# Turning a modulation row in four parts behind four row tiles instead of in one piece

## The chip, the cores and the metric

One core of a Trainium2 chip runs the whole program. The metric is the device time of one execution in microseconds; the kernel before has a median of 3093.56 us over 3 runs (3090.25 to 3096.78). Engines: PE is TensorE, DVE is VectorE, ACT is ScalarE, POOL is GpSimd, SP issues nearly all DMAs.

## The reference, cut to what matters

Two layers over 384 tokens (128 context tokens with condition `c_ctx`, 256 latent tokens with condition `c`), width 1024. Every layer has a mixer and a retrieval block; in front of and behind each stands a modulation that is a linear map of the conditions:

```python
for l in range(DEPTH):                      # 2 layers
    mp = split(silu(c_ctx) @ mod_w[l] + mod_b[l], 6)      # mod_w: (2, 1024, 6*1024)
    ms = split(silu(c)     @ mod_w[l] + mod_b[l], 6)
    hp = rms_norm(xp, norm1_g[l]) * (1 + mp[1]) + mp[0]   # the same for xs with ms
    xp = xp + mp[2] * mixer_l(hp)
    hp = rms_norm(xp, norm2_g[l]) * (1 + mp[4]) + mp[3]
    xp = xp + mp[5] * peer(hp)

def peer(x):                                # per token, 8 heads
    q = x @ wq                              # 16 halves of 128
    sv, si = top_k(q . subkeys, 16)         # 128 sub-keys, two sides per head
    fv, fi = top_k(sv0 + sv1, 16)           # 16 of the 256 pairs -> 16 of 16384 experts
    g = softmax(fv)
    return sum(g * gelu(U[idx] . x) * V[idx])
```

So twelve modulation rows of 1024 numbers (six per layer) are needed for each of the two conditions. Rows 0 to 5 serve layer 0, rows 6 to 11 serve layer 1.

## The kernel before, in words

**Retrieval without a gather.** In each layer the kernel computes U[e].x for all 16384 experts in 128 *row tiles* of 128 experts (here "tile t"), with PE as the engine in question. fp32 numbers are split in a high and a low part, and three products are added: 24 matmuls of 128 x 384 columns per tile (`s_tile`, L1213 to L1223). What feeds a tile is a chain over four engines: SP loads a tile of U into URAW; DVE transposes it into UT (`turn_u`, L1567); ACT copies the high part into UHI (`u_hi`, L860); POOL subtracts to get the low part ULO (L659); PE multiplies. ACT then applies gelu to the tile's result (`gelu`, L865), and SP stores it. UT, UHI and ULO have two buffers each, and `u_hi` of tile t+2 waits until PE is done with tile t. So each engine can be at most about two tiles ahead.

**The selection beside it.** The first 72 of the 128 tiles of a layer stand beside the *selection*: DVE finds the top 16 of the sub-key scores, for three token tiles one after the other, 24 row tiles each. DVE's selection work is written out with calls of `next_u` between, which do the transposes. After tile 17 and tile 41 PE computes the scores of the next token tile (`tile_scores`, L1198), and after tiles 29 and 53 (and 79) it transposes the picks of the last one (`turn_picks`, L1210). Behind tile 72 come the gate matmuls (`gates`, L1233), 16 passes behind each tile, and after tile 127 the stage with V (L1246).

**The modulation rows of layer 1** are computed beside the selection of layer 0 ("the first selection"). Rows 6 to 11 take 12 tiles each. A row has four *products* (`next_mod` to `mod_product`, L982): after tile 12r, 12r+3, 12r+6 and 12r+9 PE multiplies the two conditions with 256 columns of `mod_w`, 8 matmuls with 32 output rows each that use four strips of the array; the profile shows each matmul as two passes. ACT copies the result to a quarter of MROW (L690). A product leaves the numbers along a row; the kernel needs them down the partitions. That is the *turn* (`next_mod_row`, L1009 to L1017): 8 matmuls, 16 passes, with MROW as weights and a two-column selector as the moving operand, into 16 columns of bank 7. ACT copies them to MODT (L696). Before the change the whole turn stands behind tile 12r+11, and the next row's first product behind tile 12r+12.

**Order and semaphores.** The order on every engine is written out by hand. PE signals a product by s_mrow, ACT its copy by s_mev; PE signals a turn by s_mtr, ACT its copy by s_mod. A turn waits for the row's four copies and for the MODT copy of the row before. ACT's copy of the next row's first product waits for s_mtr, since it overwrites MROW. SP loads the weights of product b+2 after product b, in four DMAs of 256 KB behind three tiles (`load_next_mod`, L396). `turn_picks` waits for s_mod, since it writes to bank 7 too.

**Layer 1** has the same selection, with nothing beside it. There the 72 tiles are run by loops (`s_tiles`, L351) on PE, ACT and SP; in layer 0 they are written out.

The loop over tiles on PE, before (L1256 to L1267):

```python
def s_tiles_beside(first, count):
    if l == 0:
        for six in range(first // 6, (first + count) // 6):
            r, i = divmod(six, 2)
            for j in range(6):
                s_tile(3 * six + j // 2, j % 2)
                if j % 3 == 0:
                    next_mod(r, i, j // 3)
            if i:
                next_mod_row(r)
    else:
        s_tiles(pe, first, count, s_tile)
```

Of the kernel before, what the change touches and what calls it, by code (L numbers as in the profile page):

```python
# [34 lines left out]
KC = D // P  # L35
# [41 lines left out]


S_LEVEL1, S_LEVEL2 = 18, 6
S_PICK = 6  # L80
BATCH = 8
HALF = 64
# [51 lines left out]
def build_step(nc, x_prompt, x_sample, cache_k, cache_v, c, c_ctx, mod_w, mod_b, norm1_g, norm2_g,  # L134
# [5 lines left out]
    with ctx:  # L140
# [188 lines left out]
        LATE0 = range(LATE00 + len(BESIDE), LATE1)  # L329
        LATE2 = range(LATE1 + NBT, MODSEGS * SEGB)  # L330
        pe_names = ["hm", "kv", "ktok", "rot", "s0", "s1"]
# [34 lines left out]
        def _(sp):  # L366
# [29 lines left out]
            def load_next_mod(b, part):  # L396
                sp.dma_start(MODR[:, b % 2, 2 * part:2 * part + 2, :], mod_w[1, :, bass.ds(b * MODB, MODB)]
                             .rearrange("(p k) m -> p k m", k=KC)[:, 2 * part:2 * part + 2, :]).then_inc(next_in[b % 2], 16)
# [66 lines left out]
            for u in range(2):  # L465
                load_a_out(u)
            load_late_mod(LATE0[0] + 2, MODSEGS * SEGB)
            for u in range(2, KC):
# [32 lines left out]
            for l in range(LAYERS):  # L501
# [18 lines left out]
                for k in range(2):  # L520
                    load_v(l, k, k)
                if l == 0:
                    for k in range(2):
                        sp.wait_ge(s_mrow, MODSEGS * SEGB - 1 + k)
                        for part in range(4):
                            load_next_mod(k, part)
                for k in range(2):
# [3 lines left out]
                n = TT * (S_LEVEL1 + S_LEVEL2)  # L531
                if l == 0:
                    blocks = MODSEGS * SEGB
                    for t in range(2, n):
                        s_step(l)(t // 2, t % 2)
                        b = t // 3 + 1
                        if 2 <= b < blocks:
                            if t % 3 == 0:
                                sp.wait_ge(s_mrow, blocks + b - 1)
                                load_next_mod(b, 0)  # L540
                                load_next_mod(b, 1)
                            else:
                                load_next_mod(b, 1 + t % 3)
                else:
                    s_tiles(sp, 2, n - 2, s_step(l))
                at = n
# [116 lines left out]
        def _(act):  # L663
# [20 lines left out]

            def next_mod(r, i, k):

                row = MODSEGS + r
                act.wait_ge(s_mrow, SEGB * row + 2 * i + k + 1)
                act.wait_ge(s_mtr, row)
                nc.scalar.activation(MROW[:, bass.ds(2 * MODB * i + MODB * k, MODB)], PS[:, 2, MODB * k:MODB * k + MODB], ACT.Copy)\  # L690
                    .then_inc(s_mev, 1)

            def next_mod_row(r):

                act.wait_ge(s_mtr, MODSEGS + r + 1)
                nc.scalar.activation(MODT[:, 1, KC * r:KC * r + KC, :],  # L696
                                     PS[:, 7, MODT_AT:MODT_AT + 2 * KC].rearrange("p (a b) -> p a b", b=2), ACT.Copy).then_inc(s_mod, 1)
# [116 lines left out]
            for b, (qt, j) in enumerate(BATCHES):  # L814
                n = P if qt == 0 else T
                if b + 1 < NBT:
                    exponents(b + 1)
                mpe.wait(act, f"t{b}")
                mact.mark(f"pt{b}", nc.scalar.activation(PROBT[:, :, 0:n], PS[:, 4:8, 0:n], ACT.Copy))
                mpe.wait(act, f"o{b}")  # L820
                rows = slice(64 * j, 64 * j + 64)
                mact.mark(f"oh{b}", nc.scalar.activation(HH[rows, 0:4, qt * P:qt * P + P],
                                                         PS[rows, 4, :].rearrange("p (a b) -> p a b", a=4), ACT.Copy))
                late_mod(LATE1 + b, 5)
            for b in LATE2:
# [7 lines left out]
            for l in range(LAYERS):  # L833
# [52 lines left out]
                def s_steps_beside(first, count):  # L886
                    if l == 0:
                        for six in range(first // 6, (first + count) // 6):
                            r, i = divmod(six, 2)
                            for j in range(6):  # L890
                                s_step(3 * six + j // 2, j % 2)
                                if j % 3 == 0:
                                    next_mod(r, i, j // 3)
                            if i:
                                next_mod_row(r)
                    else:
                        s_tiles(act, first, count, s_step)

# [69 lines left out]
        def _(pe):  # L968
# [32 lines left out]

            def next_mod(r, i, k):

                row = MODSEGS + r
                pe.wait_ge(next_in[k], 64 * (2 * r + i + 1))
                pe.wait_ge(s_mev, SEGB * row + 2 * i + k - 1)
                mod_product(2, k, k * MODB)

            def next_mod_row(r):  # L1009

                row = MODSEGS + r
# [137 lines left out]
            for b, (qt, j) in enumerate(BATCHES):  # L1149
                rows = slice(64 * j, 64 * j + 64)  # L1150
                nkt = 1 if qt == 0 else 3
                if b:
                    mdve.wait(pe, f"ol{b - 1}")
                    late_mod_left(LATE1 + b - 1)
# [17 lines left out]
                late_mod(LATE1 + b, 5)  # L1172
            for b in LATE2:
# [5 lines left out]
            mdve.wait(pe, "pl3")  # L1179
            late_mod_left(MODSEGS * SEGB - 1)  # L1180
            project_out("a_out")

            for l in range(LAYERS):
# [18 lines left out]
                def turn_picks(tile):  # L1202
                    g = TT * l + tile
                    pe.wait_ge(s_pick, g + 1)
                    if l == 0:
                        pe.wait_ge(s_mod, 1 + MODSEGS + (tile + 1) * MODSEGS // TT)
                    if g:
# [48 lines left out]
                def s_tiles_beside(first, count):  # L1256
                    if l == 0:
                        for six in range(first // 6, (first + count) // 6):
                            r, i = divmod(six, 2)
                            for j in range(6):  # L1260
                                s_tile(3 * six + j // 2, j % 2)
                                if j % 3 == 0:
                                    next_mod(r, i, j // 3)
                            if i:
                                next_mod_row(r)
                    else:
                        s_tiles(pe, first, count, s_tile)  # L1267

# [51 lines left out]
        def _(dve):  # L1320
# [169 lines left out]
            for g in range(4):  # L1490
# [3 lines left out]
                                                           in1=HH[:, 4 + g, :].bitcast(F32), op0=ALU.mult, op1=ALU.subtract))  # L1494
            modulation(0, EARLY, MODSEGS)
            los("a_out")
            to_residual("a_out", 0)

            for l in range(LAYERS):
                if l:  # L1500
                    modulation(1, 0, MODSEGS)
                    lo("c_in", 0, 1)
# [67 lines left out]
                def s_step(i, k):  # L1570
                    turn_u(i + 1, k)
# [35 lines left out]
                for tile in range(TT):  # L1607
# [53 lines left out]
                    assert turned[0] == 1 + (tile + 1) * (S_LEVEL1 + S_LEVEL2)  # L1661
                if l == 0:
                    dve.wait_ge(s_mrow, 2 * MODSEGS * SEGB)

# [127 lines left out]
```

## Time and profile before

| what | value |
|---|---|
| median of 3 runs | 3093.56 us (3090.25 to 3096.78) |
| profiled execution | 3099.12 us, span 3096.7 us |
| mean granted clock of PE | 0.963 |
| PE busy | 2934.4 us, 95% |
| VectorE busy | 2022.8 us, 65% |
| ScalarE busy | 1213.9 us, 39% |
| GpSimd busy | 656.0 us, 21% |
| HBM traffic | 184 GB/s over the span |

The span runs from the first to the last instruction on the chip; the execution's own time is 2.4 us longer. Busy times are sums over instructions. The profile shows a matmul longer than its distance to the next one, since it draws the pipeline too: read starts, not lengths, for the pace. The granted clock is a share of 2.4 GHz; its two levels are 1.00 (2.4 GHz) and 0.50 (1.2 GHz), and a stretch's figure is the mean over it.

### The profile page before, as it was taken

What the parts mean: (1) busy time and instruction counts of PE and PEld (TensorE: products, weight loads), DVE (VectorE), ACT (ScalarE), POOL (GpSimd) and SP (SyncE); (2) the same over time, 40 slices, a digit from 0 to 9 for tenths busy, and PEclk for the clock granted to TensorE, in tenths of its full rate; (3) what the DMA queues carried; (4) which work ended last, traced back from release to release, by engine and by line L of the source; (5) the groups of instructions that cost most, each with busy time, mean ns of one, the idle gap of its engine ahead of it and who ended that gap; (6) DMA issues with size and microseconds to landing.
All of it is one profiled execution on the core that took longest, in us unless ns stands there. A gap on an engine that the chain in (4) does not pass through costs nothing.

```text
span 3096.7 us, 52836 instructions
## 1 busy us (share of the span) xinstructions
PE 2934.4 (95%) x15772; PEld 2632.4 (85%) x15772; DVE 2022.8 (65%) x3636; ACT 1213.9 (39%) x1639; POOL 656.0 (21%) x293
## 2 busy tenths in 40 slices
PE   4878999999999999999998989999999999999998
PEld 2646989999999978888887879999999988888886
DVE  2334477788899745555556556999989955555555
ACT  2224333333555533333333343343455533333333
POOL 0210044444333410000000003555533430000000
PEclk8869999999999999999999999999999999999999
DMA  6523476776477777777763334555467777777774
GB/s 200 153 76 95 124 196 197 213 206 186 140 204 211 214 215 225 225 225 225 223 220 94 108 95 145 165 162 175 141 187 208 206 215 224 227 223 227 224 227 131
DMA packets 508660, 569.73 MB, mean 184 GB/s; under 512 B 46584, under 2 KB 456468, under 8 KB 508564
## 3 DMA queue, kind: packets, MB, share of 16 engines
q1 hardware_dynamic: 508276, 568.43, 61.6%
q8 instruction: 46, 0.75, 0.1%
q14 instruction: 50, 0.41, 0.0%
q10 hardware_dynamic: 288, 0.13, 0.0%
HBM read 466.05 MB, written 102.37 MB: 184 GB/s over the span
## 4 chain that ended last, share of the span: by engine, by line
issue 66%; PE 19%; POOL 12%; DMA 1%; SPq 1%; POOLq 0%; DVE 0%; ACT 0%; ACTq 0%
PE PS L1246 17%; POOL ULO L659 11%; DMA MODR<-in_mod_w_dram 1%; PE PS L1042 0%; POOL AR L646 0%; POOLq L656 0%; PE PS L982 0%; SPq L424 0%; DMA RAW<-in_a_out_w_dram 0%; PE PS L998 0%; PE PS L1072 0%; POOL AR L651 0%; PE PS L1073 0%; PE PS L1074 0%; POOL AR L653 0%
## 5 line engine op out<-in xcount | busy, mean ns | idle before, releaser
L659 POOL TENSOR_TENSOR ULO<-UT,UHI 128x1024 fp32r<-128x1024 f32 x256 | 626.0, 2446 | 1746.2 <-ACT UHI L860 1746.2
L1220 PE MATMUL PS<-HH,UHI 128*128 128x384 f32 x2048 | 709.6, 346 | 25.1 <-POOL ULO L659 25.1
L1567 DVE STREAM_TRANSPOSE UT<-URAW 128x1024 f32<-128x1024 f32 x256 | 567.5, 2217 | 203.4 <-POOL ULO L659 84.9
L1221 PE MATMUL PS<-HL,UHI 128*128 128x384 f32 x2048 | 695.8, 340 | 0.0
L1222 PE MATMUL PS<-HH,ULO 128*128 128x384 f32 x2048 | 695.5, 340 | 0.0
L860 ACT ACTIVATE UHI<-UT 128x1024 fp32r<-128x1024 f32 x256 | 271.1, 1060 | 739.3 <-PE PS L1222 701.6
L1402 DVE TENSOR_TENSOR WLO<-RAW,WHI 128x1024 fp32r<-128x1024 f32 x322 | 394.3, 1225 | 239.9 <-ACT WHI L746 238.8
L1246 PE MATMUL PS<-WHI,EHI 128*128 128x512 f32 x1536 | 473.7, 390 | 3.8 <-DVE WLO L1402 3.8
L1246 PE MATMUL PS<-WHI,ELO 128*128 128x512 f32 x1536 | 473.5, 390 | 0.0
L1246 PE MATMUL PS<-WLO,EHI 128*128 128x512 f32 x1536 | 473.4, 389 | 0.0
L1220 PEld LDWEIGHTS PS<-HH,UHI 128*128 128x128 f32 x2048 | 393.7, 192 | 39.5 <-issue 31.4
L1221 PEld LDWEIGHTS PS<-HL,UHI 128*128 128x128 f32 x2048 | 393.2, 192 | 0.0
L1222 PEld LDWEIGHTS PS<-HH,ULO 128*128 128x128 f32 x2048 | 392.7, 192 | 0.0
L937 ACT ACTIVATE EHI<-SIN_ 128x384 fp32r<-128x384 f32 x256 | 134.4, 525 | 658.2 <-PE PS L1246 646.5
L1701 DVE TENSOR_TENSOR ELO<-SIN_,EHI 128x384 fp32r<-128x384 f32 x256 | 145.8, 569 | 371.5 <-ACT EHI L937 371.5
L746 ACT ACTIVATE WHI<-RAW 128x1024 fp32r<-128x1024 f32 x322 | 337.7, 1049 | 85.1 <-PE PS L1074 65.5
L1246 PEld LDWEIGHTS PS<-WHI,EHI 128*128 128x128 f32 x1536 | 288.7, 188 | 64.3 <-DVE WLO L1402 4.6
L1246 PEld LDWEIGHTS PS<-WLO,EHI 128*128 128x128 f32 x1536 | 288.6, 188 | 60.1
L1246 PEld LDWEIGHTS PS<-WHI,ELO 128*128 128x128 f32 x1536 | 288.6, 188 | 60.0
L874 ACT ACTIVATE AR<-PS 128x512 f32 x192 | 206.5, 1190 | 1.4 <-PE PS L1233 1.4
L1673 DVE TENSOR_SCALAR MODR<-IOTA,PICK 128x128 f32<-128x128 f32 x768 | 203.0, 350 | 0.0
L1233 PE MATMUL PS<-MODR 128*128 128x128 f32 x1536 | 191.5, 278 | 1.6 <-DVE MODR L1673 1.6
(185 smaller groups left out, 2840.0 us busy)
## 6 DMA issues: line engine op xcount, KB each, us to landing
URAW<-in_peer_u_dram SPq DMA_DIRECT2D x1024, 128.0 KB, 3.0
RAW<-in_peer_v_dram SPq DMA_DIRECT2D x256, 512.0 KB, 4.2
gelu_dram<-GEL SPq DMA_DIRECT2D x256, 192.0 KB, 1.9
AR<-gates_dram SPq DMA_DIRECT2D x128, 384.0 KB, 3.3
SIN_<-gelu_dram SPq DMA_DIRECT2D x256, 192.0 KB, 3.1
gates_dram<-AR SPq DMA_DIRECT2D x80, 512.0 KB, 3.6
MODR<-in_mod_w_dram SPq DMA_DIRECT2D x24, 1024.0 KB, 5.7
MODR<-in_mod_w_dram SPq DMA_DIRECT2D x96, 256.0 KB, 3.5
```

The source lines that it names most:

```text
L659: pool.tensor_tensor(ULO[k][:, :], UT[:, k, :], UHI[k][:, :].bitcast(F32), ALU.subtract).then_inc(s_ulo, 1)
L746: nc.scalar.activation(WHI[k][:, :], RAW[:, k, :], ACT.Copy).then_inc(s_hi, 1)
L860: nc.scalar.activation(UHI[k][:, :], UT[:, k, :], ACT.Copy).then_inc(s_uhi, 1)
L874: nc.scalar.activation(STAGE[half % 2][:, :, bass.ds(16 * turn + 4 * group, 4)].rearrange("p i t -> p t i"), PS[:, 3 + group, :].rearrange ...
L1220: nc.tensor.matmul(PS[:, k, 0:T], UHI[k][:, cols], HH[:, c_, :], start=c_ == 0, stop=False)
L1221: nc.tensor.matmul(PS[:, k, 0:T], UHI[k][:, cols], HL[:, c_, :], start=False, stop=False)
L1222: ins = nc.tensor.matmul(PS[:, k, 0:T], ULO[k][:, cols], HH[:, c_, :], start=False, stop=c_ == KC - 1)
L1233: ins = nc.tensor.matmul(PS[:, 3 + 2 * k + group, q * P:q * P + P], OH2[k][:, tok, :], OH1[k][:, tok, :], start=True, stop=True)
L1246: ins = nc.tensor.matmul(PS[:, 2 + 2 * tile + half, :], e[k][:, tok], w[k][:, 512 * half:512 * half + 512], start=first and q == 0, stop=l ...
L1402: V.tensor_tensor(WLO[k][:, :], RAW[:, k, :], WHI[k][:, :].bitcast(F32), ALU.subtract).then_inc(s_lo, 1)
L1567: V.transpose(UT[:, k, :].rearrange("p (c b e) -> p c b e", c=KC, b=4), URAW[:, k, :, :].rearrange("p b (j c) -> p c b j", c=KC)).then_inc ...
L1673: ins = V.tensor_scalar(OH1[k][:, j, :], IOTA[:, :], PICK[:, 0, bass.ds(first + j, 1)], PICK[:, 2, bass.ds(first + j, 1)], ALU.is_equal, A ...
```

## The change

PE's turn of a row is cut into four parts of two matmuls (four passes) each. They stand behind tiles 12r+10, 12r+11, 12r+12 and 12r+13. For the last row (row 11) the beside-work ends at tile 71, so part 0 stands behind tile 70 and parts 1, 2 and 3 behind tile 71. Part 2 of the other rows is followed at once by the next row's first product, behind the same tile. ACT copies the turned row behind tile 12r+13 and, after it, that first product's quarter of MROW (before: behind tile 12r+12). Products, their places and their loads stay where they were. A product now waits for the copy of the product before it, where it waited for the one before that.

The code is written so that both layers go through it. For layer 1 there are no rows left (`BESIDE_FIRST` is 12 at both ends), but its 72 tiles are now written out on PE, ACT and SP instead of run by loops. The waits in `turn_picks` and ahead of the one-hots exist in both layers now; in layer 1 their semaphores have long had those values. In layer 0 the values that `turn_picks` waits for are the same as before (9, 11, 13). `FRONTB` is 24, which replaces `MODSEGS * SEGB`, also 24.

```diff
+BESIDE_FIRST = (6, 12, 12)
+BESIDE_SPAN = (12, 24)
+FRONTB = BESIDE_FIRST[0] * SEGB
+
+def products_beside(l, t):
+    step = BESIDE_SPAN[l] // SEGB
+    n = t // step
+    return SEGB * BESIDE_FIRST[l] + n if t % step == 0 and n < SEGB * (BESIDE_FIRST[l + 1] - BESIDE_FIRST[l]) else None
+
+def turns_beside(l, t):
+    rows = BESIDE_FIRST[l + 1] - BESIDE_FIRST[l]
+    r, at = divmod(t + 2, BESIDE_SPAN[l])
+    if 1 <= r <= rows and at < 4:
+        row = BESIDE_FIRST[l] + r - 1
+        return [(row, part) for part in (range(1, 4) if t == LEVELS - 1 else (at,))]
+    return []
 ...
 # SP
-                if l == 0:
-                    blocks = MODSEGS * SEGB
-                    for t in range(2, n):
-                        s_step(l)(t // 2, t % 2)
 ...
-                else:
-                    s_tiles(sp, 2, n - 2, s_step(l))
+                for t in range(2, n):
+                    s_step(l)(t // 2, t % 2)
+                    for late in range(3):
+                        b = products_beside(l, t - 3 - late) if t >= 3 + late else None
+                        if b is not None and b + 2 in blocks:
+                            if late == 0:
+                                sp.wait_ge(s_mrow, b + 1)
+                                load_next_mod(b + 2, 0)
+                            load_next_mod(b + 2, late + 1)
 # ACT
+                    for t in range(first, first + count):
+                        s_step(t // 2, t % 2)
+                        for row, part in turns_beside(l, t):
+                            if part == 3:
+                                next_mod_row(row)
+                        late = t % BESIDE_SPAN[l] == 1 and t > BESIDE_SPAN[l]
+                        b = products_beside(l, t - 1 if late else t)
+                        if b is not None and (late or b % SEGB or t == 0):
+                            next_mod(b)
 # PE
-            def next_mod_row(r):
-                row = MODSEGS + r
-                pe.wait_ge(s_mev, SEGB * (row + 1))
-                pe.wait_ge(s_mod, row + 1)
-                for m in range(KC):
+            def next_mod_turn(row, part):
+                if part == 0:
+                    pe.wait_ge(s_mev, SEGB * (row + 1))
+                    pe.wait_ge(s_mod, row + 1)
+                for m in (2 * part, 2 * part + 1):
                     ins = nc.tensor.matmul(PS[:, 7, MODT_AT + 2 * m:MODT_AT + 2 * m + 2], chunk_view(MROW[:, :])[:, m, :], SEL[:, :],
                                            start=True, stop=True)
-                ins.then_inc(s_mtr, 1)
+                if part == 3:
+                    ins.then_inc(s_mtr, 1)
 ...
+                    for t in range(first, first + count):
+                        s_tile(t // 2, t % 2)
+                        for row, part in turns_beside(l, t):
+                            next_mod_turn(row, part)
+                        b = products_beside(l, t)
+                        if b is not None:
+                            next_mod(b)
```

## Rows read from the trace of the kernel before

**Rows 1.** The page, part 1: busy time, share of the span, instructions.
```profile
PE 2934.4 (95%) x15772; PEld 2632.4 (85%) x15772; DVE 2022.8 (65%) x3636; ACT 1213.9 (39%) x1639; POOL 656.0 (21%) x293
```

**Rows 2.** PE's waits, first selection (390:775) and second (1890:2215): total us, times, longest.
```profile
PE PS L1220 <- POOL ULO L659: 7.4, 2, 5.3
...
PE PS L1220 <- POOL ULO L659: 8.6, 2, 5.4
```

**Rows 3.** Timeline of PE around the first turn: start us, us, instruction.
```profile
453.22 0.34 PE L1222 MATMUL PS<-HH,ULO 128*128 128x384 f32 x1
453.39 3.80 PE L1015 MATMUL PS<-SEL,MROW 128*128 128x2 f32 x16
457.05 0.67 PE L1220 MATMUL PS<-HH,UHI 128*128 128x384 f32 x1
457.52 0.52 PE L1221 MATMUL PS<-HL,UHI 128*128 128x384 f32 x1
457.84 0.52 PE L1222 MATMUL PS<-HH,ULO 128*128 128x384 f32 x1
...
464.14 1.07 PE L982 MATMUL PS<-MODR,COND 128*32 128x256 f32 x16
```

**Rows 4.** Groups of PE in 390 to 775 us: busy us, mean ns.
```profile
L1015 PE MATMUL PS<-SEL,MROW 128*128 128x2 f32 x96 | 22.8, 368 | 0.0
```

**Rows 5.** Windows: length, busy us (x) of PE, PEld, DVE, ACT, POOL, PEclk, DMA, GB/s.
```profile
457.05:464.14 7.09, 7.09 (x25) 6.84 (x25) 5.35 (x27) 0.18 (x1) 0.38 (x1) 0.58 0.44 121
521.88:529.01 7.13, 7.13 (x25) 6.88 (x26) 3.58 (x9) 0.18 (x1) 0.10 (x1) 0.58 0.49 118
583.50:590.54 7.04, 7.04 (x25) 6.78 (x25) 5.08 (x27) 0.18 (x1) 0.09 (x1) 0.59 0.41 117
648.28:655.36 7.08, 7.08 (x26) 6.82 (x26) 3.59 (x9) 0.18 (x1) 0.10 (x1) 0.58 0.49 117
709.84:716.84 7.00, 7.00 (x26) 6.75 (x26) 5.09 (x27) 0.18 (x1) 0.10 (x1) 0.59 0.46 122
774.90:781.73 6.83, 6.83 (x26) 6.83 (x27) 3.11 (x9) 0.18 (x1) 0.10 (x1) 0.59 0.29 77
417.58:453.39 35.81, 35.81 (x228) 34.14 (x225) 29.89 (x99) 11.49 (x19) 19.22 (x8) 1.00 0.82 228
784.00:1090.00 306.00, 305.18 (x2003) 299.53 (x2002) 262.73 (x474) 171.33 (x199) 124.39 (x52) 1.00 0.71 198
...
751.69:757.50 5.81, 5.81 (x24) 5.81 (x25) 5.81 (x3) 1.26 (x2) 3.39 (x1) 0.71 0.59 175
```

**Rows 6.** Timeline of PE at the wait inside the stretch, tile 67 to 68.
```profile
749.31 0.34 PE L1222 MATMUL PS<-HH,ULO 128*128 128x384 f32 x1
751.69 0.44 PE L1220 MATMUL PS<-HH,UHI 128*128 128x384 f32 x1 [2.04 <-POOL ULO L659]
```

**Rows 7.** Timeline of PE: the tile behind the second scores, and the product behind it.
```profile
490.75 0.42 PE L1220 MATMUL PS<-HH,UHI 128*128 128x384 f32 x1
...
495.10 1.07 PE L982 MATMUL PS<-MODR,COND 128*32 128x256 f32 x16
```

**Rows 8.** Timeline of PE, second selection: first matmul and end of a run of 12 tiles.
```profile
2026.70 0.42 PE L1220 MATMUL PS<-HH,UHI 128*128 128x384 f32 x1
...
2076.71 3.73 PE L1198 MATMUL PS<-SKT,AR 128*128 128x128 f32 x32
```

**Rows 9.** Timeline of PE's weight loads at the first turn.
```profile
453.22 3.88 PEld L1015 LDWEIGHTS PS<-SEL,MROW 128*128 128x128 f32 x16
```

**Rows 10.** Timeline of ACT behind the first turn, with its idle time.
```profile
457.23 0.18 ACT L696 ACTIVATE MODT<-PS 128x16 f32<-128x16 f32 x1 [1.85 <-PE PS L1015]
...
465.64 0.38 ACT L690 ACTIVATE MROW<-PS 128x256 f32<-128x256 f32 x1
469.67 1.06 ACT L860 ACTIVATE UHI<-UT 128x1024 fp32r<-128x1024 f32 x1 [3.65 <-PE PS L1222]
```

**Rows 11.** Timeline of DVE behind the first turn: transposes of row tiles, with idle time.
```profile
467.94 2.19 DVE L1567 STREAM_TRANSPOSE UT<-URAW 128x1024 f32<-128x1024 f32 x1 [5.47 <-POOL ULO L659]
473.34 2.22 DVE L1567 STREAM_TRANSPOSE UT<-URAW 128x1024 f32<-128x1024 f32 x1 [1.69 <-POOL ULO L659]
```

More of the change, by code:

```diff
@@ L329, in build_step @@
         LATE0 = range(LATE00 + len(BESIDE), LATE1)
-        LATE2 = range(LATE1 + NBT, MODSEGS * SEGB)
+        LATE2 = range(LATE1 + NBT, FRONTB)
         pe_names = ["hm", "kv", "ktok", "rot", "s0", "s1"]
@@ L396, in load_next_mod @@
             def load_next_mod(b, part):
-                sp.dma_start(MODR[:, b % 2, 2 * part:2 * part + 2, :], mod_w[1, :, bass.ds(b * MODB, MODB)]
+                l, at = divmod(b, MODSEGS * SEGB)
+                sp.dma_start(MODR[:, b % 2, 2 * part:2 * part + 2, :], mod_w[l, :, bass.ds(at * MODB, MODB)]
                              .rearrange("(p k) m -> p k m", k=KC)[:, 2 * part:2 * part + 2, :]).then_inc(next_in[b % 2], 16)
@@ L466, in _ @@
                 load_a_out(u)
-            load_late_mod(LATE0[0] + 2, MODSEGS * SEGB)
+            load_late_mod(LATE0[0] + 2, FRONTB)
             for u in range(2, KC):
@@ L521, in _ @@
                     load_v(l, k, k)
-                if l == 0:
[L523 to L526, printed above, removed]
+                blocks = range(SEGB * BESIDE_FIRST[l], SEGB * BESIDE_FIRST[l + 1])
+                for b in blocks[:2]:
+                    sp.wait_ge(s_mrow, b - 1)
+                    for part in range(4):
+                        load_next_mod(b, part)
                 for k in range(2):
@@ L683, in mod, with next_mod, next_mod_row @@
                                          PS[:, 7, 0:2 * KC].rearrange("p (a b) -> p a b", b=2), ACT.Copy).then_inc(s_mod, 1)
-            def next_mod(r, i, k):
-                row = MODSEGS + r
-                act.wait_ge(s_mrow, SEGB * row + 2 * i + k + 1)
+            def next_mod(b):
+                row, q = divmod(b, SEGB)
+                k = b % 2
+                act.wait_ge(s_mrow, b + 1)
                 act.wait_ge(s_mtr, row)
-                nc.scalar.activation(MROW[:, bass.ds(2 * MODB * i + MODB * k, MODB)], PS[:, 2, MODB * k:MODB * k + MODB], ACT.Copy)\
+                nc.scalar.activation(MROW[:, MODB * q:MODB * q + MODB], PS[:, 2, MODB * k:MODB * k + MODB], ACT.Copy)\
                     .then_inc(s_mev, 1)
-            def next_mod_row(r):
-                act.wait_ge(s_mtr, MODSEGS + r + 1)
-                nc.scalar.activation(MODT[:, 1, KC * r:KC * r + KC, :],
+            def next_mod_row(row):
+                l, seg = divmod(row, MODSEGS)
+                act.wait_ge(s_mtr, row + 1)
+                nc.scalar.activation(MODT[:, l, KC * seg:KC * seg + KC, :],
                                      PS[:, 7, MODT_AT:MODT_AT + 2 * KC].rearrange("p (a b) -> p a b", b=2), ACT.Copy).then_inc(s_mod, 1)
@@ L823, in _ @@
                                                          PS[rows, 4, :].rearrange("p (a b) -> p a b", a=4), ACT.Copy))
-                late_mod(LATE1 + b, 5)
+                if LATE1 + b < FRONTB:
+                    late_mod(LATE1 + b, 5)
             for b in LATE2:
@@ L886, in s_steps_beside @@
                 def s_steps_beside(first, count):
[L887 to L897, printed above, removed]
+                    for t in range(first, first + count):
[7 more added lines that the diff above has]
+                            next_mod(b)
                 def picks_out(tile):
@@ L1000, in mod, with next_mod @@
                     ins.then_inc(s_mtr, 1)
[L1002 to L1006, printed above, removed]
+            def next_mod(b):
+                k = b % 2
+                pe.wait_ge(next_in[k], 64 * ((b - FRONTB) // 2 + 1))
+                pe.wait_ge(s_mev, b)
                 mod_product(2, k, k * MODB)
-            def next_mod_row(r):
-                row = MODSEGS + r
-                pe.wait_ge(s_mev, SEGB * (row + 1))
-                pe.wait_ge(s_mod, row + 1)
-                for m in range(KC):
+            def next_mod_turn(row, part):
[3 more added lines that the diff above has]
+                for m in (2 * part, 2 * part + 1):
                     ins = nc.tensor.matmul(PS[:, 7, MODT_AT + 2 * m:MODT_AT + 2 * m + 2], chunk_view(MROW[:, :])[:, m, :], SEL[:, :],
                                            start=True, stop=True)
-                ins.then_inc(s_mtr, 1)
+                if part == 3:
+                    ins.then_inc(s_mtr, 1)
             def late_mod(b, bank):
@@ L1171, in _ @@
                     scores(b + 2)
-                late_mod(LATE1 + b, 5)
+                if LATE1 + b < FRONTB:
+                    late_mod(LATE1 + b, 5)
             for b in LATE2:
@@ L1179, in _ @@
             mdve.wait(pe, "pl3")
-            late_mod_left(MODSEGS * SEGB - 1)
+            late_mod_left(FRONTB - 1)
             project_out("a_out")
@@ L1204, in turn_picks @@
                     pe.wait_ge(s_pick, g + 1)
-                    if l == 0:
-                        pe.wait_ge(s_mod, 1 + MODSEGS + (tile + 1) * MODSEGS // TT)
+                    turned = ((S_LEVEL1 + S_LEVEL2) * (tile + 1) + S_PICK - 2) // BESIDE_SPAN[l]
+                    pe.wait_ge(s_mod, 1 + min(BESIDE_FIRST[l + 1], BESIDE_FIRST[l] + turned))
                     if g:
@@ L1256, in s_tiles_beside @@
                 def s_tiles_beside(first, count):
[L1257 to L1267, printed above, removed]
+                    for t in range(first, first + count):
[5 more added lines that the diff above has]
+                            next_mod(b)
                 for tile in range(TT):
@@ L1494, in _ @@
                                                            in1=HH[:, 4 + g, :].bitcast(F32), op0=ALU.mult, op1=ALU.subtract))
-            modulation(0, EARLY, MODSEGS)
+            modulation(0, EARLY, FRONTB // SEGB)
             los("a_out")
@@ L1500, in _ @@
                 if l:
-                    modulation(1, 0, MODSEGS)
+                    modulation(1, 0, BESIDE_FIRST[1] - MODSEGS)
                     lo("c_in", 0, 1)
```

15 lines of the change are left out of this document (3 added, 12 removed).

## The prediction

> **What bounds the kernel now.** I read the page first. PE is busy 95% of the span and VectorE 65% [rows 1], so the time is the time that PE needs for its own instructions, unless something holds it. Next I read PE's waits in the two stretches where the change edits code: the first selection (390 to 775 us) and the second (1890 to 2215 us). In 385 us of the first, PE waits 7.4 us, 5.3 of them once where the stretch begins; in the second it waits 8.6 us [rows 2]. A microsecond taken out of PE's stream in the first selection is therefore a microsecond of the whole, as long as the chain that feeds PE keeps up (VectorE transposes a row tile, ScalarE and GpSimd split it).
>
> Then I looked at what that stream holds. The timeline of PE around the first turn is the view that matters [rows 3]. The reader is to see two things. First, the turn itself: 16 matmul passes of two columns each, from 453.39 to 457.05, 3.66 us. There are six of these in the stretch, 96 passes [rows 4], 22 us. Second, what stands behind it: the row tile after the turn lasts from 457.05 to the start of the next product at 464.14, 7.09 us, and its matmuls start 0.32 us apart where those before the turn start 0.17 apart. The windows say why [rows 5]: the granted clock over that tile is 0.58, so most of it runs at the lower of the two levels, 1.2 instead of 2.4 GHz. All six tiles behind a turn look so (7.09, 7.13, 7.04, 7.08, 7.00 and 6.83 us at 0.58 or 0.59). The stretch between, 417.58 to 453.39, has eight tiles and two products and a granted clock of 1.00: products, each 1.0 us long, do not make the clock fall, and nor do the gate groups behind every tile from 784 us on (clock 1.00 over 306 us). The one other fall in the stretch stands behind a wait of 2.04 us [rows 6] (clock 0.71 over the tile that follows, 5.81 us).
>
> So a turn costs PE 3.66 us, and then some 2.7 us again, because the clock falls once PE has done nothing but two-column passes for that long.
>
> **The change, part by part.** *The falls.* A tile that a break precedes and a product follows, at full clock, is the one behind the second tile's scores: 490.75 to 495.10, 4.35 us [rows 7]. The five tiles behind the turns of rows 6 to 10 of the modulation (the first five turns) are longer than that by 2.74, 2.78, 2.69, 2.73 and 2.65 us [rows 5], 13.6 us together. The change cuts each of these turns into four parts of four passes, behind four tiles in a row. At 3.66 / 16 = 0.229 us a pass, a part is 0.92 us. That is below the 1.0 us of a product and the gate groups, behind which the clock stays up, and far below 2.04 and 3.66, behind which it falls. Between two parts stands a whole tile, over 4 us of full work. I take it that all five falls go: -13.6 us. The sixth turn is different: its first part stands behind tile 70, but the other three stand together behind tile 71, because the beside-work ends there. That is 12 passes, 2.75 us, which lies between the 2.04 us and the 3.66 us behind which the clock fell. I leave that fall where it is: 0.
>
> *The turn's own passes.* Their number is unchanged. The turn now breaks the tiles' stream more often: parts 0, 1 and 3 stand alone, part 2 stands directly before a product that was a break already, so each of the five rows has two breaks more and the last row one more, 11 in all. A tile within a run takes 4.17 us ((2076.71 - 2026.70) / 12 [rows 8]), and one with a break on both sides 4.35, so a break costs at most 0.18 us: +2.0 us at most. On the other side, the first pass of a part may have its weights loaded while the tile before still streams: the last matmul of the tile starts at 453.22 and the turn's first at 453.39, no more than the usual distance, although its weights were being loaded from 453.22 [rows 3, 9]. That would hide up to 0.229 us for each of 16 further parts (15 in five rows, one in the sixth), -3.7 us at most. Nearest to the rows is the middle: -1.0 us. Ends for the range: -3.7 and +2.0.
>
> *Waits.* Part 0 waits for the row's fourth piece in MROW and for the last copy to MODT. The fourth piece is copied by ScalarE behind tile 9 and part 0 stands behind tile 10, a tile later; behind it on PE are all tiles, but the wait finds its semaphores met, as it does now at tile 11 (no turn has a wait before it [rows 2]). The product at tile 12 no longer overlaps the turn's copy: ScalarE copies the turned row and then the new product's piece behind tile 13. Behind those two on ScalarE stands the next split of a tile. They take 0.18 and 0.38 us [rows 10], and ScalarE idles 3.65 us before that split, in wait for PE: hidden. If that cover were gone, 0.56 us per row, 3 us. SP issues the same loads at the same tiles; each tile now comes 2.7 us sooner per row, and PE has no wait for the weights of a product today [rows 2], which are asked for a tile earlier than they are used. I cost this at nothing.
>
> *Other layer.* In the second selection nothing stands beside the tiles, yet PE's, ScalarE's and SP's loops over it are now written out, 72 tiles. PE does a tile per 4.17 us inside the loops [rows 8]; written out, in the first selection, eight tiles and two products take 35.81 us [rows 5], 4.23 us a tile after the products' 2.0. The difference is what products cost as breaks. So neither form shows a cost: 0, with +-1 us for the range. The Trainium skill, "Runtime: NRT & Kernel Launch", section "Instruction fetch mechanics", holds that a taken branch breaks the sequential fetch and that unrolled code is preferred; by that the second selection would gain. The loops of this trace pay nothing that is seen, so the sum has nothing from it.
>
> *Sum.* 3099.1 us is the profiled execution (span 3096.7), 5.6 us above the median of 3093.56. -13.6 - 1.0 = -14.6. The profiled execution would come out at 3084.5; the median at **3079.0 us**.
>
> **What is late next.** The chain that feeds PE. VectorE mixes transposes with selection work, and in three places (tiles 18 to 22, 42 to 46, 66 to 69) that work is so dense that the 2.04 us wait arises in the third. If VectorE needs the slow tile at 12, 36 and 60 to get ahead for those places, what is won there is lost again. Against it: between the slow tile and the dense place VectorE waits for PE's side, 5.47 and 1.69 us before two transposes after the first turn [rows 11], so it had already been held back to PE's pace before the dense place begins.
>
> **The rivals.**
> 1. *The falls stay.* Part 2 and the product behind tile 12 stand together, 0.92 + 1.00 = 1.9 us of thin work, near the 2.04 us wait behind which the clock fell [rows 6]. For it: that closeness. Against it: products by themselves seem to count as work. The clock then still falls once per row, at tile 13: only the -1.0 is left, 3092.6 us. The same time comes out if the falls have to do with something other than the turn's passes. The Trainium skill, "TensorE: Matmul & The Clock Gate", section "Why this matters for your kernels", ties falls to stretches in which PE idles; in a turn PE issues a pass each 0.23 us and never idles in the trace, so by that rule taken literally the turn isn't the cause and cutting it wins nothing. Six falls behind six turns speak against that reading. Chance 8%.
> 2. *The sixth fall goes too,* because 2.75 us is short enough: a further 6.83 - 4.35 = 2.5 us, 3076.5 us. Chance 12%.
> 3. *The chain takes it back* at the three dense places: 2.74 + 2.69 + 2.65 = 8.1 us return as waits for GpSimd, 3087.1 us. Chance 6%.
> 4. *Slower: a single part is enough for a fall.* Its place is each part that stands alone, its price 2.7 us per tile at the lower clock, and it decides as soon as 0.92 us of two-column passes makes the clock fall where 1.0 us of product does not. Parts come a tile apart, so the tiles 11 to 14 would all run low where one does now: three more at 2.7, 8.2 us a row, 41 us in five rows and 2.5 in the sixth: 3093.6 + 43.6 - 1.0 = 3136 us. For it: passes of two columns do less than products do. Against it: the tiles between are full work. Chance 3%.
>
> **How the numbers follow.** Forecast 68%, rivals 12, 8, 6 and 3%, and 3% for what I haven't thought of. The likeliest case's own range is -17.3 - 1 to -11.6 + 1, and falls elsewhere come and go between executions (the runs shown lie 6.5 us apart): 3074 to 3085. Rival 3 and cases in which some of the five falls stay reach to 3089, and rival 2 to 3073: range 3073 to 3089. A measurement of this kernel tells 0.2%, 6.2 us, from no change, so faster is below 3087.4 and slower above 3099.8. Faster: 68 + 12 + half of rival 3 and a quarter of rival 1 (falls gone in some rows), 0.85. Slower: 0.05. The rest, 0.10, is the same.
>
> **What would show it.** In the trace after: 96 two-column passes as before, in groups of four of some 0.9 us with a tile between, and one group of 12; a granted clock of 1.00 from the first product to the dense place at tile 67, but for no tile at 0.32 us a step; tiles between parts of 4.2 to 4.4 us; PE's busy time in the first selection less by some 15 us and the waits for ULO as before; the second selection within 1 us. Wrong if the tile behind a part shows 0.58, if waits for ULO rise by several microseconds, or if the stages behind the first selection get longer by what it saves.

## The result, and the profile after

The changed kernel takes 3076.27 us in the median of 5 runs (3072.44 to 3083.90), the kernel before 3093.56 us (5 runs). The ratio is 0.9940, with a 95% interval of 0.9927 to 0.9953: 17.3 us faster, where 14.6 were forecast (3079.0 us). The profiled execution of the changed kernel happens to be its slowest, 3083.9 us with a span of 3082.1.

First the stretch in which the time should go. Windows (length, busy us and count of PE, PEld, DVE, ACT, POOL, PEclk, DMA share, GB/s) from the start of tile 1 to the first gate matmul; before:

```profile
403.86:781.68 377.82, 375.78 (x2266) 356.17 (x2263) 303.41 (x716) 123.88 (x190) 177.49 (x72) 0.94 0.70 200
```

and after, with two tiles behind parts of the first turn, and the tile behind the last group:

```profile
409.34:770.06 360.72, 359.12 (x2267) 340.16 (x2264) 302.57 (x716) 123.39 (x190) 181.77 (x72) 1.00 0.73 209
455.44:459.71 4.27, 4.27 (x25) 4.27 (x26) 4.24 (x15) 0.89 (x2) 2.41 (x1) 1.00 0.65 203
466.67:470.94 4.27, 4.27 (x28) 4.27 (x25) 3.15 (x12) 0.00 (x0) 1.92 (x1) 1.00 0.68 199
764.17:770.01 5.84, 5.84 (x25) 5.84 (x26) 4.13 (x10) 0.18 (x1) 1.08 (x1) 0.71 0.38 122
```

377.82 us have become 360.72: 17.1 us in this pair of executions, about what the medians differ by. The granted clock of the stretch has gone from 0.94 to 1.00. A tile between two parts takes 4.27 us at the full clock where the tile behind a turn took 7.0 to 7.1 at 0.58 [rows 5]. Only behind the group of twelve passes does the clock still fall, and the tile takes 5.84 us instead of 6.83.

The timeline of PE at the first turn, after, is the answer to [rows 3]:

```profile
454.63 0.94 PE L1035 MATMUL PS<-SEL,MROW 128*128 128x2 f32 x4
455.44 0.42 PE L1242 MATMUL PS<-HH,UHI 128*128 128x384 f32 x1
...
459.71 0.94 PE L1035 MATMUL PS<-SEL,MROW 128*128 128x2 f32 x4
460.52 0.42 PE L1242 MATMUL PS<-HH,UHI 128*128 128x384 f32 x1
...
464.79 0.95 PE L1035 MATMUL PS<-SEL,MROW 128*128 128x2 f32 x4
465.67 1.07 PE L1002 MATMUL PS<-MODR,COND 128*32 128x256 f32 x16
466.67 0.44 PE L1242 MATMUL PS<-HH,UHI 128*128 128x384 f32 x1
...
470.94 0.95 PE L1035 MATMUL PS<-SEL,MROW 128*128 128x2 f32 x4
471.75 0.42 PE L1242 MATMUL PS<-HH,UHI 128*128 128x384 f32 x1
```

Read start to start, the four parts take 0.81, 0.81, 0.88 and 0.81 us, 3.31 in all where the whole turn took 3.66. At 464.79 part 2 and the product stand together for 1.88 us, and the clock stays up over the tile behind them (466.67 to 470.94 in the windows above; the same tile of the other four rows takes 4.27 us at 1.00 too).

PE's waits in the two selections, after, answer to [rows 2]:

```profile
PE PS L1242 <- POOL ULO L678: 6.9, 2, 5.3
...
PE PS L1242 <- POOL ULO L678: 8.5, 2, 5.3
```

The first line is 390 to 775 us, the second 1875 to 2200, since the second selection starts earlier now.

Why is the profiled span only 14.6 us shorter when the stretch gives 17.1? The stretch starts later: PE's first tile starts at 401.2 us, before at 395.9. In a second profile of the same kernel it starts at 396.7, so this is variation between executions. From the first gate matmul to the end the changed kernel is 3.0 us shorter in this pair (2312.0 against 2315.0 us), of which the second selection has 0.3 (below). The stretch itself starts 5.5 us later, and 17.1 - 5.5 + 3.0 = 14.6.

### The profile page after: what moved, and what is told of

It reads as the page before. It is cut to its first block, busy times and chain, and to the rows that moved or that the text cites. A ratio compares the mean times of both kernels' runs of the same rounds, so it can differ in the third digit from the quotient of the medians.

```text
span 3082.1 us, 51618 instructions
## 1 busy us (share of the span) xinstructions
PE 2916.7 (95%) x15772; PEld 2616.0 (85%) x15772; DVE 2020.7 (66%) x3636; ACT 1213.7 (39%) x1639; POOL 660.5 (21%) x293
## 4 chain that ended last, share of the span: by engine, by line
issue 65%; PE 19%; POOL 12%; DMA 1%; SPq 1%; POOLq 0%; DVE 0%; ACT 0%; ACTq 0%
PE PS L1268 17%; POOL ULO L678 11%; DMA MODR<-in_mod_w_dram 1%; POOL AR L665 0%; PE PS L1063 0%; POOLq L675 0%; PE PS L1002 0%; DMA RAW<-in_a_out_w_dram 0%; SPq L448 0%; PE PS L1018 0%; DMA RAW<-in_peer_v_dram 0%; PE PS L1093 0%; POOL AR L670 0%; PE PS L1094 0%; PE PS L1095 0%
## 5 line engine op out<-in xcount | busy, mean ns | idle before, releaser
L1242 PE MATMUL PS<-HH,UHI 128*128 128x384 f32 x2048 | 702.5, 343 | 23.8 <-POOL ULO L678 23.8
L1585 DVE STREAM_TRANSPOSE UT<-URAW 128x1024 f32<-128x1024 f32 x256 | 566.9, 2215 | 186.4 <-POOL ULO L678 73.4
L1244 PE MATMUL PS<-HH,ULO 128*128 128x384 f32 x2048 | 688.4, 336 | 0.0
L1243 PE MATMUL PS<-HL,UHI 128*128 128x384 f32 x2048 | 687.7, 336 | 0.0
L1244 PEld LDWEIGHTS PS<-HH,ULO 128*128 128x128 f32 x2048 | 386.5, 189 | 0.0
```

What stands on the lines that cost most here:

```text
L1242: nc.tensor.matmul(PS[:, k, 0:T], UHI[k][:, cols], HH[:, c_, :], start=c_ == 0, stop=False)
L1243: nc.tensor.matmul(PS[:, k, 0:T], UHI[k][:, cols], HL[:, c_, :], start=False, stop=False)
L1244: ins = nc.tensor.matmul(PS[:, k, 0:T], ULO[k][:, cols], HH[:, c_, :], start=False, stop=c_ == KC - 1)
L1585: V.transpose(UT[:, k, :].rearrange("p (c b e) -> p c b e", c=KC, b=4), URAW[:, k, :, :].rearrange("p b (j c) -> p c b j", c=KC)).then_inc ...
```

## The experiments

Each kernel ran in five rounds beside the kernel before on its chip. The median of the kernel before lay between 3093.6 and 3099.5 us on these occasions, so ratios are compared. The stretch from tile 1 to the first gate matmul is read from each kernel's profile.

### Layer 1's loops put back

```diff
 def s_tiles_beside(first, count):
+    if l:
+        s_tiles(pe, first, count, s_tile)
+        return
     for t in range(first, first + count):
```

(the same on ScalarE and SP)

> The changed kernel, but the second selection's 72 tiles are run by loops again on PE, ScalarE and SP, as before the change. Theory (the gain is the five clock falls behind the turns and a fraction of the sixth): the same as the changed kernel within 2 us, 17 us below the kernel before; second selection within 1 us of both. Rival (writing the second selection out brought part of it): 3 us or more slower than the changed kernel, with the difference in the second selection.

Measured: 3081.28 us against 3099.43, ratio 0.9942 (0.9928 to 0.9955), the changed kernel's own ratio being 0.9940. Windows over tiles 12 to 71 of the second selection, in the order kernel before, changed kernel, this one:

```profile
1947.38:2211.24 263.86, 260.66 (x1511) 258.71 (x1511) 252.92 (x582) 99.82 (x136) 148.94 (x60) 0.99 0.54 164
```

```profile
1933.58:2197.12 263.54, 260.34 (x1511) 258.75 (x1511) 252.32 (x582) 99.89 (x136) 149.09 (x60) 0.99 0.55 165
```

```profile
1929.83:2193.73 263.90, 260.68 (x1512) 258.69 (x1512) 252.50 (x582) 99.87 (x136) 149.08 (x60) 0.99 0.55 164
```

0.3 us in 60 tiles is all that writing the loops out can be worth here. The first selection's stretch is 360.73 us in this kernel, the changed kernel's to a hundredth.

### The turn whole again, in the new code

```diff
 def turns_beside(l, t):
     r, at = divmod(t + 2, BESIDE_SPAN[l])
-    if 1 <= r <= rows and at < 4:
+    if 1 <= r <= rows:
-        return [(row, part) for part in (range(1, 4) if t == LEVELS - 1 else (at,))]
+        return [(row, part) for part in {1: (0, 1, 2, 3)}.get(at, ())]
```

(ScalarE's copies of the products at their old places)

> The changed kernel with each turn whole again behind tile 12r+11, all else (layer 1 written out, the stricter waits) as changed. Theory: the time of the kernel before, 3093.6 within 3 us, and six falls of the granted clock behind six turns, the tile behind each near 7 us. Rival (something else in the new code wins): well below 3090.

Measured: 3095.39 us against 3099.43, ratio 0.9988 (0.9979 to 0.9997). The windows show the old picture, tile behind the second turn included:

```profile
405.33:781.71 376.38, 374.33 (x2267) 354.77 (x2264) 305.23 (x719) 123.95 (x190) 177.51 (x72) 0.95 0.70 200
522.14:529.12 6.98, 6.98 (x26) 6.73 (x26) 3.59 (x9) 0.18 (x1) 0.10 (x1) 0.59 0.51 124
```

All six turns have their fall. The one at the first turn was shorter than before in this execution (its tile took 5.95 us instead of 7.09), which is 1.1 of the 1.4 us in the stretch. The medians are 4.0 us apart, and the interval of the ratio leaves out 1. The kernel of the experiment above, whose turns are cut, is 18.2 us below the same kernel before, so 14.1 of these hang on the cut. Most of the gain is the cut's, and what makes the other 4 us is open: the stretch has 1.4 of them in the profiles and the second selection 0.3.

### Halves

```diff
-        return [(row, part) for part in (range(1, 4) if t == LEVELS - 1 else (at,))]
+        return [(row, part) for part in {0: (0, 1), 1: (2, 3)}.get(at, ())]
```

> The turn in two halves of eight passes, behind tiles 12r+10 and 12r+11, in all six rows; none beside a product. A half lasts some 1.75 us, between the 0.8 us part behind which the clock stays up and the 2.7 us group behind which it fell for 3.4 us. Theory in its plain form (a longer stretch of two-column passes makes the fall): if 1.75 us is short enough, no falls at all, also not behind the last row, and 1 to 2 us less than the changed kernel (one fall of half a tile's price, 1 us, and a break fewer per row): 3075 us. If 1.75 us is enough for a fall, one of 3.4 us behind some of the twelve halves, some 1 to 1.7 us each: 3085 to 3095 us.

Measured: 3078.67 us against 3099.43, ratio 0.9931 (0.9917 to 0.9944). Windows over the stretch and over the tile behind the first half:

```profile
406.49:767.89 361.40, 359.36 (x2266) 339.76 (x2263) 299.07 (x720) 123.94 (x190) 176.04 (x72) 1.00 0.72 208
453.61:457.87 4.26, 4.26 (x25) 4.26 (x26) 4.22 (x10) 0.00 (x0) 2.03 (x1) 1.00 0.70 221
```

A half lasts 1.76 us, and behind none of the twelve does the clock fall, the last row's included. Expected was 1 to 2 us less than the changed kernel; the stretch is 0.7 us longer (361.40 against 360.72). The last row gives 1.6 us, since its fall is gone. Against it stand 1.5 us, since this kernel still has the wait of 2.04 us ahead of tile 68 with its fall and the changed kernel has not (below), and 0.8 us that the expectation lacked: two halves take 3.52 us where four parts take 3.31, since fewer first passes are hidden, and the one break fewer doesn't make up for it (0.16 us more per row).

### Twelve passes together in every row

```diff
-        return [(row, part) for part in (range(1, 4) if t == LEVELS - 1 else (at,))]
+        return [(row, part) for part in {0: (0,), 1: (1, 2, 3)}.get(at, ())]
```

> One part of four passes behind tile 12r+10 and the other twelve passes together behind tile 12r+11, in all six rows, as the changed kernel has it in the last row alone. Theory: each row falls as the last row of the changed kernel did, once, for 3.4 us (tile 5.8 us instead of 4.35) or for 6.8 (tile near 7): five further falls of 1.5 to 2.7 us, 3084 to 3091 us. Rival (the fall of the last row came from the end of the beside-work, not from the twelve passes): 3077 us, with a fall behind the last row alone.

Measured: 3084.11 us against 3099.43, ratio 0.9952 (0.9938 to 0.9966). The stretch takes 364.74 us. Windows over the tiles behind the first and the third group of twelve:

```profile
457.02:461.39 4.37, 4.37 (x26) 4.12 (x26) 3.00 (x11) 0.18 (x1) 1.35 (x1) 1.00 0.76 225
577.92:583.87 5.95, 5.95 (x26) 5.69 (x26) 5.83 (x26) 0.18 (x1) 1.05 (x1) 0.71 0.56 166
```

The same 2.71 us of passes, the same code: once no fall, once a fall of 1.6 us' price. In this execution, the fastest of its five, it fell behind two of six groups (the third and the fifth, and not the last, so the end of the beside-work is not what makes it); in the three profiles of kernels with one such group (the changed kernel twice and the one with layer 1's loops) behind all three. I expected a fall in each row. At 2.71 us it came behind some groups and not behind others with the same code around them, and what decides between them is not shown.

### The same turn with 128 columns

```diff
-nc.tensor.matmul(PS[:, 7, MODT_AT + 2 * m:MODT_AT + 2 * m + 2], chunk_view(MROW[:, :])[:, m, :], SEL[:, :],
-                 start=True, stop=True)
+nc.tensor.matmul(PS[:, 7, 384:512], chunk_view(MROW[:, :])[:, m, :],
+                 SELP[:, 14 - 2 * m:14 - 2 * m + 128], start=m == 0, stop=m == KC - 1)
```

(SELP is the selector with zeros around it; each turn whole behind tile 12r+11)

> Each turn whole again behind tile 12r+11, but with a moving operand of 128 columns instead of 2 (zeros around the selector, the eight matmuls added up in one bank half), the same weights. The weights' loading sets the pace of a turn (0.238 us a pass, while a pass of 128 columns takes 0.11 us elsewhere), so the turn keeps its 3.66 us. Theory (the clock falls because hardly a column streams for 3.66 us): no falls behind turns, each tile behind one 4.35 us instead of 7.1: 16 us below the kernel before. Rival (long weight loads or the break itself make the fall): falls as before the change, the time of the kernel before.

Measured: 3071.91 us against 3099.49, ratio 0.9913 (0.9900 to 0.9927). This is the experiment that bears most directly on the mechanism. Windows over the stretch, the first turn, and the tile behind it:

```profile
403.30:763.64 360.34, 358.70 (x2266) 338.52 (x2263) 303.39 (x716) 123.91 (x190) 178.19 (x72) 1.00 0.72 209
452.82:456.49 3.67, 3.67 (x17) 3.67 (x17) 3.67 (x3) 1.44 (x2) 1.99 (x1) 1.00 0.85 270
456.49:460.85 4.36, 4.36 (x26) 4.11 (x25) 4.29 (x17) 0.18 (x1) 0.37 (x1) 1.00 0.62 194
```

The turn lasts 3.67 us as before, in one piece, with the same weights. 128 columns stream per pass instead of 2, and the clock stays up: no fall at any of the six, 4.36 us for the tile. (The eight matmuls also add up in one region instead of writing eight; that this makes no difference to the clock was not tried by itself.) The stretch gains 17.5 us: six falls, and the same 1.5 us at the dense place as in the changed kernel. The median gains 27.6 us, more than the stretch. In its profile each gate stage takes 302.1 us from tile 76 to the stage with V, where the other profiles have 304.1 to 306.4. It stays open whether that belongs to the change.

### Weights side by side

```diff
-nc.scalar.activation(MROW[:, MODB * q:MODB * q + MODB], PS[:, 2, MODB * k:MODB * k + MODB], ACT.Copy)
+nc.scalar.activation(MROW.rearrange("p (c m) -> p m c", c=KC)[:, 32 * q:32 * (q + 1), :],
+                     PS[:, 2, MODB * k:MODB * k + MODB].rearrange("p (m c) -> p m c", c=KC), ACT.Copy)
 ...
-chunk_view(MROW[:, :])[:, m, :]
+MROW[:, P * m:P * m + P]
```

> Each turn whole behind tile 12r+11 with two columns, but ScalarE writes MROW so that the 128 weights of a matmul lie side by side instead of 32 bytes apart. Theory: if the distance is what makes a load 0.238 us, a pass takes 0.11 us as for other loads, a turn 1.8 us instead of 3.66; that is as short as the halves, behind which the clock stayed up. 6 x 1.85 = 11 us from the turns and 16 from the falls: 27 us below the kernel before. Rival (two-column passes take 0.238 us whatever the weights' layout): turns of 3.66 us with their falls, the time of the kernel before.

Measured, turn whole: 3067.71 us against 3099.49, ratio 0.9896 (0.9881 to 0.9911). Timeline of PE at the first turn, then windows over the stretch and the tile behind that turn, then the group of ScalarE's copies to MROW:

```profile
453.24 1.84 PE L1035 MATMUL PS<-SEL,MROW 128*128 128x2 f32 x16
454.94 0.42 PE L1242 MATMUL PS<-HH,UHI 128*128 128x384 f32 x1
```

```profile
403.78:753.63 349.85, 347.81 (x2267) 328.17 (x2263) 303.39 (x716) 130.17 (x190) 176.10 (x72) 1.00 0.74 215
454.94:459.28 4.34, 4.34 (x26) 4.09 (x25) 4.27 (x12) 0.36 (x2) 2.38 (x1) 1.00 0.89 254
```

```profile
L709 ACT ACTIVATE MROW<-PS 128x256 f32<-128x256 f32 x24 | 15.4, 644 | 0.0
```

and the same group in the kernel before:

```profile
L690 ACT ACTIVATE MROW<-PS 128x256 f32<-128x256 f32 x24 | 9.0, 376 | 0.0
```

The turn takes 1.70 us instead of 3.66, from start to start, and no fall stands behind any turn. ScalarE pays 0.27 us more per copy, hidden. Expected 27 us, measured 31.8 in the median and 28.0 in the stretch; the 3.8 us between them are of the size of the 4 us that the whole turn in the new code was faster by, and as open.

### Both: packed and in halves

The edits of the last kernel and of the halves together.

> Both: weights side by side, and the turn in two halves behind tiles 12r+10 and 12r+11. Theory: halves of 0.8 us without falls; 11 us from the turns and 16 to 18 from the falls, less 1 us for the further breaks: 26 to 29 us below the kernel before, within 1.5 us of the packed whole turn. Rival (the packed whole turn still falls here and there): up to 10 us better than the packed whole turn.

Measured: 3068.27 us against 3099.49, ratio 0.9898 (0.9882 to 0.9913); a second time, on another occasion:

> The kernel with packed weights and half turns again, on the same chip as the one with all rows packed. 31 us below the kernel before, as in its first run, within 3 us.

3067.03 us against 3094.41, ratio 0.9909 (0.9894 to 0.9923). The stretch takes 350.73 and 349.40 us. The difference is one fall: both wait 2.04 us ahead of tile 68, and the clock falls behind that wait in the first profile and not in the second. Cutting the packed turn adds nothing: at 1.7 us there is no fall left to avoid. Both packed kernels are faster than the changed kernel, whose own second run gave:

> The changed kernel itself, to be compared with the others on the same chip. Theory: 17 us below the kernel before; no fall of the clock behind the five turns in parts, and a fall of 3.4 us or none behind the group of twelve passes of the last row (it has fallen in two of two profiles here, but in the kernel with twelve passes in every row in two of six rows).

3079.55 us against 3099.49, ratio 0.9931 (0.9918 to 0.9945); its stretch takes 360.71 us and has the one fall behind the last twelve passes. So the packed turn, whole and at its old place, is 12 us better than the changed kernel on the same chip.

### All twelve rows packed

> The kernel with packed weights and half turns, and the six turns of layer 0's rows (two before the projections, four beside projections and attention) packed too. Each of the six has 3.56 us between its first and last pass now, and 1.8 packed. Theory: where PE is what the stretch waits for, 1.85 us each comes off, up to 11 us; the front waits much for DMAs and other engines and is at the lower clock half of its time anyway, so part of it is lost in waits: 3 to 11 us below the kernel with six packed rows. Rival (the front is held by its DMAs alone): no difference within 2 us.

Measured: 3065.99 us against 3094.41, ratio 0.9905 (0.9888 to 0.9922), beside 0.9909 for six packed rows on the same chip. The rival holds: no difference. The first tile starts at 397.6 us where it starts at 398.2, and PE is busy 295.25 us of the front instead of 299.73: what the turns save there turns into waiting. (The expectation puts the front at the lower clock for half of its time; its granted clock is 0.84, which is a third.)

## Why the prediction was right

The steps, against what the runs showed:

- **PE is the path.** Held. The stretch shrank by 17.1 us and the median by 17.3; PE's waits for ULO are 6.9 us after 7.4.
- **The falls, -13.6 us.** Held in full. Behind none of the twenty parts of the first five rows does the clock fall; each row's tile is back from 7.0 to 7.1 us to that of a normal break. The reading of the cause also held, and no longer rests on the place alone: the wide turn has the same length, place and weights, and its clock stays up. One detail of it was off. The prediction has the clock fall once the 3.66 us are over, but the window over the first turn of the kernel before shows it below 1.00 already:

```profile
453.39:457.05 3.66, 3.66 (x17) 3.66 (x17) 3.66 (x3) 1.44 (x2) 1.98 (x1) 0.89 0.96 276
```

At two levels, 0.89 means that the last 0.8 us of the turn ran at the lower one, so the fall began after some 2.8 us of two-column passes.
- **The sixth fall, 0.** Right that it stays, off by 1.0 us in its size: the tile takes 5.84 us where it took 6.83. Nine groups of this length in four profiles had five falls, so a price for either outcome would have fitted better, and that the last group fell in all three profiles with one group is partly luck for the forecast.
- **The turn's passes, -1.0 us (-3.7 to +2.0).** Measured -1.0. A row has 3.31 us in four parts for 3.66 (-0.35), two more breaks of 0.11 us (4.27 a tile against 4.16 to 4.17), and a tile between part 1 and part 2 that takes 4.27 us instead of the 4.35 of a tile ahead of a product (-0.08): -0.2 us a row. The first pass of each part does hide behind the tile before it, by 0.14 us: the twelve passes that a whole turn has more than a part take 3.66 - 0.81 us, 0.238 each, and four at that pace would be 0.95 instead of 0.81. That the forecast hit is luck: it was the middle between two bounds, and nothing spoke for the middle.
- **The rest of the stretch, 0.** This is the term I lacked: 17.1 - 13.6 - 1.0 - 1.0 leaves 1.5 us, and tile by tile they lie at the dense place, tiles 65 to 69. The kernel before waits 2.04 us there and pays a fall behind it [rows 5, 6]; the changed one waits 1.60 us, two tiles earlier, and the clock stays up. It is no chance of one execution: all three profiles with four parts have the shorter wait, as has the wide turn, and all others the longer one. Why the order of the turns decides this was not traced.
- **Rival 1** (the falls stay because part 2 and the product stand together) is refuted by the windows at 466.67. The rule that stands beside it, from the Trainium skill, "TensorE: Matmul & The Clock Gate", section "Why this matters for your kernels", names idle gaps of PE as what to avoid; taken as the only cause it doesn't fit these traces, for PE need not idle for the clock to fall. Twelve turns of two-column passes without a gap, in two kernels, brought twelve falls.
- **Rival 2** did not come, **rival 3** was not seen (the waits did not rise), and **rival 4** was far off: 0.8 us never made a fall.
- **Layer 1's written-out loops, 0.** Shown by putting them back. The prediction has the second selection gain by the Trainium skill, "Runtime: NRT & Kernel Launch", section "Instruction fetch mechanics"; it left out that the page has a fetch stall only for a branch whose target is not among the instructions already fetched. No such stall is seen here: 60 tiles take 263.9 us in loops and 263.5 written out.

So the forecast's terms and the run agree on 14.6 us, and 2.5 us more came: 1.0 from the sixth fall and 1.5 from the dense place. The time came out inside the range because the first five falls, which carry it, were read rightly. The 4 us of the second experiment stand beside this account unexplained.

How long the stretches without a full tile were, and at how many of them the clock fell, over all profiles of this study:

| what PE does without a tile | length | falls |
|---|---|---|
| part of four two-column passes, or of eight packed ones | 0.8 us | none |
| part 2 and a product | 1.88 us | 0 of 15 |
| packed turn, or half a turn | 1.70 to 1.76 us | 0 of 18 |
| twelve passes | 2.71 us | 5 of 9 |
| whole turn | 3.66 us | 12 of 12 |
| whole turn, 128 columns | 3.67 us | 0 of 6 |
| wait at the dense place | 1.60 to 1.64 us | 0 of 4 |
| wait at the dense place | 2.04 us | 7 of 8 |

## What to carry to other kernels

Matmuls with two columns cost TensorE twice here: their own time, which halved with the weights' layout and did not change with the number of columns, and the lower clock of the dense work behind them, at every turn of 3.66 us in one piece, at some groups of 2.71 and at none of 1.76 or less. Look for tiles that take longer than their like, read the granted clock over them, and look at what stands in front. Then ask first why the thin stretch is long, and only then where to cut it: here the weights' layout was worth 28 us in the stretch, with the turn whole at its old place, and the cut 17.

## What the runs showed of the hardware that I had not expected

- **Weights 32 bytes apart load at less than half the pace.** 16 passes take 3.67 us with them (128 columns, granted clock 1.00) and 1.70 us with weights side by side. I had taken 0.229 us a pass for the price of a two-column pass as such.
- **Columns that compute nothing were free here, and more than free.** 126 further columns per pass, all zeros, left the turn at 3.67 us, whose pace the spread weights set, and saved the falls.
- **When VectorE and GpSimd work at the same time, either can be the slow one.** At the dense place GpSimd's subtract and VectorE's comparison overlap. In the kernel before, the comparison was slow and the subtract beside it was not:

```profile
737.19 2.39 POOL L659 TENSOR_TENSOR ULO<-UT,UHI 128x1024 fp32r<-128x1024 f32 x1 [2.97 <-ACT UHI L860]
737.90 3.83 DVE L1636 TENSOR_TENSOR AR<-AR,ROWAT 128x2048 f32<-128x2048 f32 x1
```

and in the changed kernel it took 2.25 us, while two of GpSimd's subtracts together took 6.87 us instead of twice 2.4, and PE waited for them. What the two engines compete for, no run here shows:

```profile
728.00 2.25 DVE L1654 TENSOR_TENSOR AR<-AR,ROWAT 128x2048 f32<-128x2048 f32 x1
```

```profile
727.99 6.87 POOL L678 TENSOR_TENSOR ULO<-UT,UHI 128x1024 fp32r<-128x1024 f32 x2 [2.98 <-ACT UHI L882]
```

```profile
732.52 0.44 PE L1242 MATMUL PS<-HH,UHI 128*128 128x384 f32 x1 [1.60 <-POOL ULO L678]
```
